# Remainders of down weights: by a subtraction on VectorE, or by a transfer that adds onto a negated copy

## What is computed

```python
def sqrelu_mlp(h, w1, w2):
    return jnp.square(jax.nn.relu(h @ w1)) @ w2
...
    h_lat = h_lat + mod_l[5] * sqrelu_mlp(modulate(rmsnorm(h_lat, norm2_g[i]), mod_l[3], mod_l[4]),
                                          mlp_w1[i], mlp_w2[i])
...
return rmsnorm(h_lat, final_g)
```

## Time and profile before

| | us |
|---|---|
| median of 3 runs | 1765.21 (1762.92 to 1766.98) |
| the profiled execution | 1765.43 |
| its span in the trace | 1763.8 |
| PE busy | 1739.3 |
| DVE busy | 1207.2 |
| ACT busy | 834.9 |
| POOL busy | 313.7 |

### The profile page before, as it was taken

How to read it: one execution, slowest core, us unless ns; L and a number is a source line. 1 busy time by engine, 2 the same in 40 slices (tenths; PEclk the granted TensorE clock), 3 DMA queues, 4 the chain that set the end, 5 groups by cost and what they waited for, 6 DMA issues and landing times.

```text
span 1763.8 us, 26282 instructions
## 1 busy us (share of the span) xinstructions
PE 1739.3 (99%) x9132; PEld 1464.9 (83%) x9132; DVE 1207.2 (68%) x1668; ACT 834.9 (47%) x1270; POOL 313.7 (18%) x368
## 2 busy tenths in 40 slices
PE   7999999999999999999999999999999999999998
PEld 4888888888888888888888888889998788999997
DVE  5788777775346666578855665686656787667764
ACT  4566666665322222365313544665534474444443
POOL 0111111110001110022111225111110412222211
PEclk8999999999999999999999999999999999999999
DMA  9343333332545563326555663111122413332221
GB/s 327 100 132 120 120 120 109 115 112 84 169 142 190 190 190 119 108 95 208 186 191 177 191 224 112 52 48 49 38 77 67 142 41 138 105 102 96 96 83 50
DMA packets 76245, 221.12 MB, mean 125 GB/s; under 512 B 9328, under 2 KB 19952, under 8 KB 76144
## 3 DMA queue, kind: packets, MB, share of 16 engines
q1 hardware_dynamic: 56800, 160.20, 27.5%
q0 software_dynamic: 17632, 56.83, 10.6%
q10 hardware_dynamic: 1712, 2.75, 0.5%
HBM read 217.52 MB, written 2.23 MB: 125 GB/s over the span
## 4 chain that ended last, share of the span: by engine, by line
PE 85%; DVE 6%; DVEq 4%; ACT 3%; DMA 1%; issue 1%; ACTq 0%; POOLq 0%; POOL 0%; SPq 0%
PE bank L448 15%; PE bank L449 15%; PE bank L450 15%; PE bank L1256 3%; PE bank L1258 3%; PE bank L1257 3%; PE bank L2286 3%; PE bank L2287 3%; PE bank L2288 3%; PE bank L2259 2%; PE bank L2261 2%; PE bank L2260 2%; DVEq L1156 1%; PE bank L1307 1%; PE bank L1308 1%
## 5 line engine op out<-in xcount | busy, mean ns | idle before, releaser
L434 DVE TENSOR_TENSOR wlo<-wraw,whi 128x1024 fp32r<-128x1024 f32 x250 | 313.8, 1257 | 129.3 <-ACT whi L414 108.7
L414 ACT ACTIVATE whi<-wraw 128x1024 fp32r<-128x1024 f32 x218 | 230.2, 1058 | 327.9 <-PE bank L450 219.3
L448 PE MATMUL bank<-uhi,whi 128*128 128x512 f32 x916 | 359.0, 392 | 0.0
L450 PE MATMUL bank<-uhi,wlo 128*128 128x512 f32 x916 | 356.6, 389 | 0.0
L449 PE MATMUL bank<-ulo,whi 128*128 128x512 f32 x916 | 356.4, 389 | 0.0
L450 PEld LDWEIGHTS bank<-uhi,wlo 128*128 128x128 f32 x916 | 172.0, 188 | 36.1
L448 PEld LDWEIGHTS bank<-uhi,whi 128*128 128x128 f32 x916 | 172.0, 188 | 35.2
L449 PEld LDWEIGHTS bank<-ulo,whi 128*128 128x128 f32 x916 | 172.0, 188 | 34.7
L1032 POOL DMA_DIRECT2D aring<-in_ada x160 | 86.0, 538 | 423.6 <-DVE aacc L1046 219.3
L448 PE MATMUL bank<-vhi,whi 128*128 128x512 f32 x408 | 159.7, 391 | 0.4 <-DVE vlo L1153 0.4
L450 PE MATMUL bank<-vhi,wlo 128*128 128x512 f32 x408 | 158.8, 389 | 0.0
(11 more groups left out here) (496 smaller groups left out, 3534.6 us busy)
## 6 DMA issues: line engine op xcount, KB each, us to landing
wraw<-in_units SPq DMA_DIRECT2D x252, 512.0 KB, 3.8
aring<-in_ada POOLq DMA_DIRECT2D x160, 256.0 KB, 3.7
qsrc<-in_units SPq DMA_DIRECT2D x28, 512.0 KB, 4.6
slab<-in_ada SPq DMA_DIRECT2D x32, 256.0 KB, 7.4
es<-decay_rows POOLq DMA_DIRECT2D x32, 256.0 KB, 4.6
eac<-decay_rows POOLq DMA_DIRECT2D x32, 128.0 KB, 3.0
x<-in_xT SPq DMA_DIRECT2D x4, 512.0 KB, 6.1
xr<-in_xT ACTq DMA_DIRECT2D x1, 2048.0 KB, 11.9
```

The source lines that it names most:

```text
L414: act.activation(whi[:, at % SLOTS, :], wraw[:, at % RAW, :], ACT.Copy).then_inc(w_hi, 1)
L434: dve.tensor_tensor(wlo[:, at % SLOTS, :], wraw[:, at % RAW, :], whi[:, at % SLOTS, :].bitcast(f32), ALU.subtract).then_inc(w_split, 1)
L448: pe.matmul(out, wh, rhs_hi(k), start=first and k == 0, stop=False)
L450: mm = pe.matmul(out, wl, rhs_hi(k), start=False, stop=last and k == KT - 1)
```

## The change

For the way-down pairs of the second MLP, DVE's subtraction is taken out. ACT makes two parts: hi as before, and -hi into `wlo` (a copy with scale -1.0); after that it raises `w_split`. A new function `pair_rest` on POOL waits for `w_split` and issues a transfer of the same weights, from the same place in memory, with the operation "add": it adds the weights onto -hi, which leaves the remainder in `wlo`. The way-down steps of PE wait for this transfer (on `ada_ld{n % 4}`) instead of for `w_split`. POOL's first sums wait for "tlo" 3 instead of 2, and POOL's order mixes sums and transfers. In SP's order the load of pair 2g + 5 goes behind `quad_top` (for g = 0 behind `quad_low` as well).

```diff
@@ mlp2_loads (SP)
             for g in range(QUADS):
-                pair_load(sp, 2 * g + 5)
                 if g + 2 < QUADS:
                     q_wait(sp, "done", PRODUCTS * g + 3)
                     quad_top(sp, g + 2)
+                if g > 0:
+                    pair_load(sp, 2 * g + 5)
                 if g + 2 < QUADS:
                     q_wait(sp, "done", PRODUCTS * g + 7)
                     quad_low(sp, g + 2)
+                if g == 0:
+                    pair_load(sp, 5)
                 if 2 * g + 6 < 32:
                     pair_load(sp, 2 * g + 6)
@@ mlp2_pool
-            q_wait(pool, "tlo", 2)
-            for g in range(1, QUADS):
+            pair_rest(pool, 0)
+            pair_rest(pool, 1)
+            q_wait(pool, "tlo", 3)
+            quad_sums(pool, 1)
+            pair_rest(pool, 2)
+            pair_rest(pool, 3)
+            pair_rest(pool, 4)
+            for g in range(2, QUADS):
                 quad_sums(pool, g)
+                pair_rest(pool, 2 * g + 1)
+                pair_rest(pool, 2 * g + 2)
+            for n in (29, 30, 31):
+                pair_rest(pool, n)
@@ pair_hi (ACT)
-                act.activation(whi[:, at % SLOTS, :], wraw[:, at % RAW, :], ACT.Copy).then_inc(w_hi, 1)
-
-        def pair_lo(dve, n):
+                act.activation(whi[:, at % SLOTS, :], wraw[:, at % RAW, :], ACT.Copy)
+                act.activation(wlo[:, at % SLOTS, :], wraw[:, at % RAW, :], ACT.Copy, scale=-1.0).then_inc(w_split, 1)
+
+        def pair_rest(pool, n):
             if n < 32:
-                lo_part(dve, M0 + 4 + n, 0)
+                at, (unit, col) = M0 + 4 + n, down_pair(n)
+                pool.wait_ge(w_split, at + 1)
+                pool.dma_start(wlo[:, at % SLOTS, :].rearrange("p (a n) -> p a n", a=2),
+                               units[unit:unit + 3:2, :, col:col + 512].rearrange("a p n -> p a n"),
+                               accum_op=ALU.add).then_inc(N2[f"ada_ld{n % 4}"], 16)
@@ down_ready (PE)
-            at = M0 + 4 + 2 * g + i // 2
-            pe.wait_ge(w_split, at + 1)
+            n = 2 * g + i // 2
+            at = M0 + 4 + n
+            pe.wait_ge(N2[f"ada_ld{n % 4}"], 640 + 16 * (n // 4 + 1))
@@ mlp2_dve, mlp2_period_dve
-            pair_lo(dve, ...)        (all 32 calls)
```

More of the change, by code:

```diff
@@ L2435, in mlp2_dve @@
             turned_dve(dve, 3)
-            pair_lo(dve, 0)
             first_tile_dve(dve, 3)
@@ L2441, in mlp2_dve @@
             quad_lo(dve, 4)
-            pair_lo(dve, 1)
             turned_lo(dve, 2)
@@ L2452, in mlp2_dve @@
             quad_lo(dve, 7)
-            pair_lo(dve, 2)
             down_dve(dve, 0, 1)
@@ L2457, in mlp2_dve @@
             down_dve(dve, 0, 2)
-            pair_lo(dve, 3)
             quad_lo(dve, 10)
-            pair_lo(dve, 4)
             quad_lo(dve, 11)
@@ L2465, in mlp2_dve @@
             down_dve(dve, QUADS - 1, 3)
-            pair_lo(dve, 31)
             for i in range(4):
@@ L2488, in mlp2_period_dve @@
             y_added_dve(dve, g)
-            pair_lo(dve, 2 * g + 3)
             down_dve(dve, g, 0)
@@ L2501, in mlp2_period_dve @@
                 quad_lo(dve, at + 9)
-            pair_lo(dve, 2 * g + 4)
             if more:
```

## The result

The changed kernel takes 1773.66 us (median of 5 runs, 1770.10 to 1775.10) beside 1765.21 for the kernel before (5 runs): a ratio of 1.0053, 95% interval 1.0040 to 1.0065. By the ratio it is slower by 9.4 us (7 to 11.5), and the two medians lie 8.5 us apart, where 1.2 was forecast, with a range that ended at 1772.0.

A forecast was written before the change was run, and what follows sets the result against it. PE was taken to bound the kernel (busy 1739.3 of 1763.8 us). A new stall of +4.3, +0.1 for restart and -3.2 for three holes gave +1.2: 1765.2 to 1766.4 us, range 1763.0 to 1772.0.

The forecast's parts named there:

- the steady periods: From 1478.36 us on: periods stay at 21.04 us, ACT's extra copies cost nothing, transfers have 28 and 31 us of cover.
- L: Time from issue to landing of an adding transfer: taken as 7.0 us for pair 0, ends 3.8 and 10.2.
- the wait for pair 0: PE idle at the stage's first way-down step until pair 0's transfer lands: 4.3 us, plus 0.1 for the restart.
- S: PE's stall at the first way-down step: L - 2.7, so 4.3 us for L = 7.0.
- the neighbour: Plain load released by the same semaphore step as pair 0's transfer, sharing the DMA engines: adds 1.6 us to L.
- the second read: An adding transfer reads two operands, the weights and ScalarE's part: 1.6 us on top of a plain load's 3.8.
- the early holes: PE's holes before 1446.31 (DVE's remainder of an up weight) and 1451.37 (DVE's addition): both go, 1.4 us.
- POOL, which must issue it first, is free: Pair 4, copied by 1459.8, doesn't delay POOL's sums: there at 1466.5, DVE asks at 1469, 2.5 us of cover.
- the third hole: PE's hole before 1474.09, from an up load held in SyncE's queue: goes with the new load order, 1.7 us.
- A: Rival: the adding transfer lands like a plain one, L 3.8 to 5.4, 1763.2 to 1764.8 us; chance 0.12.
- B: Rival: the addition is slow on the DMA engines, deciding at pair 0 from L = 9.3; 1769.6 to some 1788; chance 0.22.
- C: Rival: PE's seventh product still waits, now behind ACT's longer chain; holes stay beside the stall, up to 1769.6 us; chance 0.08.

## Why the prediction was wrong, step by step

**Right: the steady periods.** 28 to 31 us of cover were enough. From the third period's start to the end the two kernels differ by 0.02 us, though ACT and POOL carry more. Pair 31, too, was hidden: 6.1 us of flight against 11.5 of cover.

**Right: L and the wait for pair 0.** L was put at 7.0 and measured at 7.0 (6.7 to 7.5 in the kernels with the same order). The wait was S + 0.1 = 4.4, and PE starts 4.40 us late. That it came out to the tenth is in part luck, since the terms were sized otherwise: the neighbour at 1.6, measured 1.1 (7.1 against 6.0); the second read at 1.6, measured 1.4 together with the addition. The rest is the flight of a plain transfer by POOL with the neighbour, 5.7, where my terms made 3.8 + 1.6 = 5.4.

How much work a transfer is for the 16 DMA engines can be read from one row of the profile's page, whose last number is a queue's share of their time; it is the row that grows when POOL issues the 32 transfers. The kernel before, the one with plain transfers and the changed one:

```profile
q0 software_dynamic: 17632, 56.83, 10.6%
...
q0 software_dynamic: 26336, 73.61, 13.9%
...
q0 software_dynamic: 26336, 73.61, 16.4%
```

Each share is of its own span (1763.8, 1766.1 and 1768.1 us). By my estimate from these rows, one of the 32 plain transfers takes 1.8 us of all engines and an adding one 3.2. The Trainium skill ("Collectives: The Full Stack", section "The bandwidth ceiling: the fold count and why AG ≠ RS ≠ AR") puts a reducing transfer at half the rate because of its two source reads; it says so of rings of three or more ranks. The engines' time here comes near that (3.2 against 1.8), while the flight grows by a third (4.7 to 6.1), by the same 1.4 us. Alone, the adding transfer took 6.0 us, where the prediction made 5.4 of that rule.

**Nearly right: the early holes.** They were to go, with 1.4 us. The first did, and of the second 0.23 us of idle time is left, so 1.02 us came back.

**Wrong: "POOL, which must issue it first, is free".** This is the step on the third hole. Issuing pair 4 held POOL for 1.2 us, as priced, and the first sum began at 1460.23. But POOL's own `drain()` between the sums then waited for the landing. The second sum began 9.4 us after the first, and the sums that were to be there at 1466.5 (33.4 us after the start of the stage) reached DVE at 1472.30 (43.7 after it). A part of that was harmless: ACT's copies of pair 4 were over 30.5 us after the start, where the prediction had 26.7, and POOL began that much later. The kernel without drains has the same late start (30.5), has the three sums 36.4 us after the start, and no hole. The margin was 2.5 us ("each microsecond over these 2.5 us of cover would come back"); the drain took 7.64. The idle time of 1.43 us, which was to go, became 3.80. I had read `drain()` as a wait for arithmetic and gave no price to a transfer in flight ahead of it, though no row of mine showed that pairing; it should have been bounded from both sides, by nothing and by the rest of the flight. The trace of the kernel before has one place of that kind, which I hadn't looked for: POOL issues six small transfers, makes a first sum, drains, and stands for 1.81 us where the next drain costs it 0.17. It goes on 0.7 us after the last of the six has landed (1068.4), so this place hints at the wait and doesn't show it.

```profile
1069.13 0.74 POOL L2613 TENSOR_TENSOR cacc<-cacc,csq 128x256 f32<-128x256 f32 x1 [1.81 <-issue]
1070.04 1.74 POOL L2613 TENSOR_TENSOR cacc<-cacc,csq 128x256 f32<-128x256 f32 x1 [0.17 <-issue]
```

The kernel without drains and the one with the sums first each take the hole away, by different edits. The landing plus 0.2 to 0.3 us meets the start of the second sum in the changed kernel (twice) and in all five experiments that keep the drains (at least twice each). A drain of the last norm waits as well, for pair 31 (landed 1743.79), and costs nothing:

```profile
1744.13 1.29 POOL L2097 TENSOR_TENSOR nt<-nt,nsq 128x512 f32<-128x512 f32 x1 [3.71 <-issue]
```

**Wrong: a stall costs what PE waits.** The sum had 0.1 us for a restart, from the rows of holes of 0.35 to 1.43 us. Behind the stalls of 4.25 and 3.80 us the clock was at half, for 1.44 and 1.58 us more. The kernel that fills the stall with matmuls shows this as a cost of its own (2.84 instead of 5.29 us). The Trainium skill ("TensorE: Matmul & The Clock Gate", section "Why this matters for your kernels") warns of idle gaps between bursts of matmuls for this reason. The trace agrees (0.50 behind both stalls), and I should have weighed it, since my own forecast had a stall three times as long as any that the rows showed.

In the terms of the prediction, with what was measured. The prediction has one term of -3.2 for the three holes; the rows of PE before, set against a period of 21.04 us, split it into 1.4, 1.7 and 0.1 (the restart behind the third).

| term | forecast | measured |
|---|---|---|
| stall for pair 0, with restart | +4.4 | +4.40 |
| clock behind it | 0 | +1.44 |
| two early holes | -1.4 | -1.02 |
| third hole | -1.7 | +2.39 |
| restart and clock behind it | -0.1 | +1.58 |
| sum | +1.2 | +8.79 |

So 4.1 of the 7.6 us missed are the drain's hole, 3.1 the clock, and 0.4 what is left of the early holes.

**The rivals.** A (lands like a plain one) fell, though not far: even a plain transfer gave 1.0014. B (a slow addition, deciding from L = 9.3 at pair 0) had the right sign and the wrong mechanism: flights of 9.9 us did occur and did hurt, but at pair 4, through the drain, not at pair 0. C (the relief isn't turned into time because ACT's chain is longer) wasn't it: no hole of the changed kernel ends at ACT. No rival had a place for a wait in POOL's own program, and this was the one that decided.

What stays open: why pairs 1 to 4 of the changed kernel take 7.6 to 9.9 us to land against a median of 6.1. SyncE's loads share the engines there (shares of 0.93 to 1.11 between 1460 and 1466 us). The kernel with the sums first speaks for this sharing: there pair 4 goes out at 1471.20, behind the last of those loads, and lands after 5.7 us instead of 9.9. As a change of its own I tested it for pair 0 alone.

## What to carry to other kernels

A transfer moved onto an engine's queue has to be costed against every barrier in that engine's program, not only against its instructions: here an engine stood at the drain behind it until it had landed, for up to 9 us, and a wait on a counting semaphore in its place cost nothing. When a change makes PE wait for several microseconds where it never did, add the matmuls that follow at half the clock: behind stalls of 2.3 to 4.7 us that came to 1.4 to 2.8 us. And take a change of several parts to pieces: the reorder of SyncE's loads was the whole gain (0.1%, give or take as much), and the transfers that it came with bring nothing that can be measured even when PE waits for none of them.

## What the runs showed of the hardware

- GpSimd's `drain()` waits until the transfers that it issued have landed, adding or plain. It stood 4.17, 7.64, 4.26, 9.11 and 3.57 us in the rows above, each time until 0.2 to 0.3 us after a landing, and not at all once the drain was a semaphore wait.
- In this stage the granted clock fell to 0.50 with idle stretches of PE of 2.31, 2.94, 3.06, 3.18, 3.80, 4.25, 4.34 and 4.74 us, and stayed at 1.00 behind those of 0.65, 1.43 and 1.72. When it fell, and when it came back, varied: for 2.31, 3.18 and 3.80 us it fell only 0.9 to 1.5 us after PE was back at work. A step of 12 full-width matmuls (2.73 us) took 4.06 to 5.29 behind a wait for a transfer.
- A transfer of 512 KB that adds takes 6.1 us to land against 4.7 for a plain one on the same queue (medians of 32), and holds GpSimd for 1.20 us to issue against 0.72. It takes some 3.2 us of all 16 DMA engines against 1.8 (estimated from the shares of their queue).
- GpSimd's sums and VectorE's two-input steps slow each other: 2.83 us for a step of 0.69, 1.78 for the sum of 1.29 beside it.
